# Hymba decoder step: compression weights in 2 KB runs with strided page transposes, input tiles behind earlier page units

## The chip, the core and the metric

The kernel runs on one core of one Trainium2 chip. Its engines are TensorE (PE; its weight loads are shown as PEld), VectorE (DVE), ScalarE (ACT), GpSimd (POOL) and SyncE (SP); SP, ACT and POOL also issue transfers (DMAs). The metric is device time in microseconds of one execution; lower is better. Times are compared by the medians of several executions, and the trace is of one profiled execution.

## The reference

One decoding layer for a prompt of 512 tokens and for 8 sequences of 8 new tokens, each with 2048 cached tokens in 16 pages. The layer is an adaLN-modulated RMSNorm, one input projection, attention with three branches (compressed blocks, selected blocks, window) beside a gated short convolution, an output projection and a SwiGLU network. The part that matters here is the compression of the cached keys and values, over all pages of each sequence:

```python
def compress(rows, pe, w1, w2):
    b, t = rows.shape[:2]
    r_n = CMP_LEN // CMP_STRIDE
    n_ch = t // CMP_STRIDE
    nc = n_ch - r_n + 1
    chunks = rows[:, :n_ch * CMP_STRIDE].reshape(b, n_ch, CMP_STRIDE, N_KV_HEADS, HEAD_DIM)
    chunks = chunks.transpose(0, 1, 3, 2, 4).reshape(b, n_ch, N_KV_HEADS, CMP_STRIDE * HEAD_DIM)
    proj = jnp.einsum('bnkf,rfh->rbnkh', chunks, w1.reshape(r_n, CMP_STRIDE * HEAD_DIM, CMP_HIDDEN))
    pre = sum(proj[r][:, r:r + nc] for r in range(r_n)) + pe.reshape(-1) @ w1
    return jax.nn.silu(pre) @ w2, jnp.arange(nc) * CMP_STRIDE + CMP_LEN - 1
```

`w1` is `w_ck1` for keys and `w_cv1` for values, 2048 x 64 each; `pe` is `pe_cmp`, 32 x 64; `CMP_LEN` is 32 and `CMP_STRIDE` 16 tokens.

## The kernel before

The kernel is written by hand for all five engines: each engine has one list of instructions that it runs in order, and the lists meet through semaphores. There is no planner at run time; the order in the text is the order on each engine.

**Page units.** The cached rows come in 16 units (`caches`, u = 0 to 15): for each of 8 sequences the keys (even u) and the values (odd u), 1 MB each. GpSimd fetches a unit with four indirect DMAs (L891) into one of four slots of `cring`, a part of `arena`. Before the first DMA of unit i (i at least 4) it waits until `turned` has reached i - 3, that is, until the transposes of units 0 to i - 4 have been made. VectorE then transposes the unit in blocks of 32 x 32 (`turn_chunks`, L1605, one instruction of 2048 elements a partition) into `xcmp`, of which there are two. TensorE multiplies it with `w1v` (`compress_first`, L2513: eight products that accumulate), ScalarE copies one half of the result (`second_chunks`, L1058), VectorE adds the other half (`both_chunks`, L1611), ScalarE applies SiLU (`hidden`, L1066), TensorE makes the second product (`compress_second`, L2521) and VectorE evicts it (`cmp_evac`, through L1528).

**The page loop.** For u = 0 to 15 VectorE transposes unit u + 1, evicts the second product of unit u - 2 and makes the addition for unit u. The transpose of unit u + 2 waits for TensorE's first product of unit u. Between these stand other steps: at u = 0 the evictions of the small transposed rows and of the position sums `pebt`; at u = 7 and 8 the normalisation of the input tiles; at u = 8 to 10 evictions of the transposed tiles; at u = 12 the addition of the adaLN bias (L1563); at u = 13 the modulation (L1552 to L1585, right before the addition for unit 13); at u = 14 the low part of the projection's first weights (L535). TensorE has between the units also eight steps of the adaLN product (`ada_step`, u = 4 to 11) and transposes of the input tiles. After unit 15 the input projection begins (L2445 to L2455), for which ScalarE and VectorE split weights into high and low parts.

**The position term** `pe.reshape(-1) @ w1` is made by `position_rows` after unit 0's first product: 32 products with one column each (L2501; two instruction pairs in the trace for each), with columns 36 to 51 of `colT`. These come from `pe_cmp`, which is loaded in rows of `rowb` with gains and convolution weights and transposed with them (`turn_rows`).

**Loads at the start.** ScalarE issues the identity (L1020), then `hidden_load(0)` (`w_ck1`), the gain rows, the position rows, `hidden_load(1)` (`w_cv1`), `w2` and the convolution state; only then does it run the SiLU on the condition vectors (L1049). Each `hidden_load` is eight DMAs of 64 KB, with runs of one row of 64 values (256 bytes); the row of `w1` with which partition p goes is fixed by the 32 x 32 transposes: partition 32 i + p holds feature 32 (8 i + j) + p for each j. TensorE waits for `comp_k_loaded` before unit 0 and for `comp_w_loaded` before the position sums.

SP issues the page table and the condition vectors, then the loop of L762 to L766 quoted below: it waits for page unit 2 before the first tile of x and for unit 3 before the second. `cache(eng, i)` is a wait for the four DMAs of unit i. The first four 1 MB chunks of the adaLN weights follow (L718), and then the further chunks, each behind the step that frees its place in the ring of four.

## Time and profile before

| | us |
|---|---|
| three runs | 916.96, 919.9, 920.78 |
| median | 919.9 |
| profiled execution, first to last instruction (span) | 917.5 |
| median less span (launch and what else lies around; the profiled execution's own time is not listed apart) | 2.4 |
| TensorE busy in the span | 851.0 (93%) |
| VectorE busy in the span | 624.0 (68%) |
| page stretch: first page DMA to the projection's first product | 4.15 to 127.19 |

The page is read from the top: span, busy time of each engine, then the 40 slices of the span, of which the first five or six are the page stretch. A busy share over the whole span says little here, since the page stretch and the later products have different limits; what counts for this change is which wait ends last between 4 and 127 us. In a line of the timeline the number behind the start is how long the instruction, or the row of neighbours of one kind that is merged into one line, was busy; in brackets stands how long the engine had been idle before, and what released it. "remote" means that the profile found no releaser; "issue" that the engine waited for nothing that it shows.

### The profile page before, as it was taken

Reading aid. Unit: us, or ns where it says so; the run is one execution under the profiler, and the core shown is the slowest. Engines: PE = TensorE matmul, PEld = TensorE weight load, DVE = VectorE, ACT = ScalarE, POOL = GpSimd, SP = SyncE. Lnnn points to the kernel's source line nnn. Section 1 sums busy time; section 2 is a strip of 40 time slices with the busy share of each in tenths; the row PEclk is TensorE's granted clock in tenths of the full one; section 3 lists DMA queues with packets and bytes.
Section 4 is the critical chain, followed back from the end, with each engine's and each line's share of the span. In section 5 each row is a group of like instructions: output and inputs, shape, how many; then the busy total and the mean of one; then the engine's idle time right before and its main releaser. Section 6 shows DMA issues by size and latency. Waiting matters only on the chain.

```text
span 917.5 us, 17109 instructions
## 1 busy us (share of the span) xinstructions
PE 851.0 (93%) x6685; PEld 725.8 (79%) x6685; DVE 624.0 (68%) x1220; ACT 374.3 (41%) x754; POOL 307.3 (33%) x303
## 2 busy tenths in 40 slices
PE   3499999999997789999999998999999999999998
PEld 2366778899994456776777798999999999888886
DVE  2146686388948674668485899988888888434444
ACT  1033262132135434866833664444444446323221
POOL 6456500000003311634400328766677773000000
PEclk9699999999998887999999999999999999999999
DMA  7988922237187987393102554333333324422201
GB/s 207 323 293 320 321 79 75 92 111 262 45 299 259 351 337 275 87 303 108 36 0 92 152 139 123 92 94 92 92 94 93 93 92 165 145 92 93 74 1 52
DMA packets 89167, 138.88 MB, mean 151 GB/s; under 512 B 9268, under 2 KB 59988, under 8 KB 84799
## 3 DMA queue, kind: packets, MB, share of 16 engines
q1 hardware_dynamic: 74866, 96.26, 32.6%
q0 software_dynamic: 9376, 40.31, 12.7%
q10 hardware_dynamic: 4844, 1.21, 0.6%
q8 instruction: 54, 0.88, 0.4%
q14 instruction: 27, 0.21, 0.1%
HBM read 130.58 MB, written 11.31 MB: 155 GB/s over the span
## 4 chain that ended last, share of the span: by engine, by line
PE 74%; DVE 10%; issue 8%; ACT 4%; POOL 2%; another core or an unknown queue 1%; DVEq 0%; POOLq 0%; ACTq 0%
PE bank L2445 17%; PE bank L2447 17%; PE bank L2446 16%; PE bank L2513 4%; PE bank L2439 4%; PE bank L2801 2%; PE bank L2474 2%; PE bank L2714 2%; PE bank L2933 2%; PE bank L2454 2%; PE bank L2455 2%; PE bank L2965 2%; PE bank L2771 1%; DVE ring_lo L535 1%
## 5 line engine op out<-in xcount | busy, mean ns | idle before, releaser
L2445 PE MATMUL bank<-s,ring_hi 128*128 128x288 f32 x620 | 184.1, 297 | 4.5 <-DVE ring_lo L535 4.5
L2446 PE MATMUL bank<-s,ring_lo 128*128 128x288 f32 x620 | 182.9, 295 | 0.0
L2447 PE MATMUL bank<-s,ring_hi 128*128 128x288 f32 x620 | 182.3, 294 | 0.0
L2445 PEld LDWEIGHTS bank<-s,ring_hi 128*128 128x128 f32 x620 | 116.2, 187 | 5.4 <-DVE ring_lo L535 5.3
L2447 PEld LDWEIGHTS bank<-s,ring_hi 128*128 128x128 f32 x620 | 116.8, 188 | 0.0
L2446 PEld LDWEIGHTS bank<-s,ring_lo 128*128 128x128 f32 x620 | 116.4, 188 | 0.0
L535 DVE TENSOR_TENSOR ring_lo<-mem,ring_hi 128x512 fp32r<-128x512 f32 x84 | 106.6, 1304 | 2.1 <-POOL mem L987 1.8
L535 DVE TENSOR_TENSOR dn_w<-wring,dn_w 128x2048 fp32r<-128x2048 f32 (+1 forms) x11 | 23.1, 2097 | 65.8 <-ACT dn_w L532 65.8
L2445 PE MATMUL bank<-dn_w,dn_hi 128*128 128x512 f32 x160 | 62.2, 389 | 0.0
L2446 PE MATMUL bank<-dn_w,dn_lo 128*128 128x512 f32 x160 | 62.2, 389 | 0.0
L2447 PE MATMUL bank<-dn_w,dn_hi 128*128 128x512 f32 x160 | 62.2, 389 | 0.0
L900 POOL DMA_INDIRECT arena<-in_cache_k_slc,idx x8 | 7.9, 991 | 162.0 <-PE bank L2447 152.0
L2445 PE MATMUL bank<-hhi,ws 128*128 128x288 f32 x192 | 56.8, 296 | 0.0
L2447 PE MATMUL bank<-h1hi,ws 128*128 128x288 f32 x192 | 56.6, 295 | 0.0
L2446 PE MATMUL bank<-h1hi,ws 128*128 128x288 f32 x192 | 56.5, 294 | 0.0
L532 ACT CAST dn_w<-wring 128x2048 fp32r<-128x2048 f32 (+1 forms) x11 | 19.3, 1757 | 83.0 <-PE bank L2447 83.0
L535 DVE TENSOR_TENSOR ring_lo<-wring,ring_hi 128x512 fp32r<-128x512 f32 x71 | 52.6, 746 | 0.5 <-ACT ring_hi L532 0.5
L532 ACT CAST ring_hi<-mem 128x512 fp32r<-128x512 f32 x84 | 50.0, 616 | 6.9 <-POOL mem L979 2.3
L979 POOL TENSOR_TENSOR mem<-wring 128x512 f32<-128x512 f32 x20 | 27.1, 1357 | 53.8 <-PE bank L2447 30.1
L532 ACT CAST ws<-wring 128x1024 fp32r<-128x1024 f32 (+2 forms) x18 | 21.8, 1247 | 48.4 <-PE bank L2455 27.2
L891 POOL DMA_INDIRECT arena<-in_cache_k_cmp,idq x32 | 30.6, 955 | 28.0 <-DVE uvT L1605 15.1
L532 ACT CAST ring_hi<-wring 128x512 fp32r<-128x512 f32 x71 | 39.8, 616 | 0.0
(448 smaller groups left out, 2127.4 us busy)
## 6 DMA issues: line engine op xcount, KB each, us to landing
wring<-in_w_gu SPq DMA_DIRECT2D x44, 512.0 KB
wring<-in_w_ada SPq DMA_DIRECT2D x16, 1024.0 KB
wring<-in_w_in SPq DMA_DIRECT2D x10, 1024.0 KB
wring<-in_w_down SPq DMA_DIRECT2D x10, 1024.0 KB
wring<-in_w_ada SPq DMA_DIRECT2D x16, 512.0 KB
proj<-in_x_prompt SPq DMA_DIRECT2D x4, 512.0 KB
mem<-in_state_k_win POOLq DMA_DIRECT2D x8, 256.0 KB
mem<-in_state_v_win POOLq DMA_DIRECT2D x8, 256.0 KB
```

The source lines that it names most:

```text
L532: return copy(dst, src)
L535: return eng.tensor_tensor(dst, src, hi.bitcast(F32), ALU.subtract)
L891: pool.indirect_dma_start(cring[:, slot_of(i), 512 * n:512 * n + 512], None, a[name].rearrange("l n (c i s) k d -> (l n c i) (s k d)", i=4 ...
L979: ins = pool.tensor_tensor(dst, block_of(f, 0), block_of(f, 1), ALU.subtract)
L2439: return pe.transpose(dst, src, ident[0:P, 0:P])
L2445: pe.matmul(dst, sh, ml, start=first and k == 0, stop=False)
L2446: pe.matmul(dst, sl, mh, start=False, stop=False)
L2447: ins = pe.matmul(dst, sh, mh, start=False, stop=last and k == len(pairs) - 1)
L2454: pe.matmul(dst, s, ml, start=first and k == 0, stop=False)
L2455: ins = pe.matmul(dst, s, mh, start=False, stop=last and k == len(pairs) - 1)
L2474: ins = pe.matmul(ps(key)[32 * j:32 * j + 32, :], cT[:, 32 * kk:32 * kk + 32], w[:, j, :], start=kk == 0, stop=kk == 7)
L2513: ins = pe.matmul(dst, w1v[:, u % 2, j].rearrange("p r h -> p (r h)"), x[:, j // 2, j % 2], start=j == 0, stop=j == 7)
```

## The change

1. `hidden_load(x)` becomes one DMA of 512 KB into a new place `w1_rows` (a part of `late`), with runs of 512 values (2 KB): partition p now gets the eight consecutive rows 8 p to 8 p + 7 of each half r. A new step `hidden_place(x)` on ScalarE waits for it and copies it into `w1v` in the order that TensorE reads. Both copies stand behind the SiLU on the condition vectors.
2. For this order of the features a page's values have to be transposed with a stride: element j of each run of 8 goes to product j. `turn_chunks` makes eight instructions of 256 elements a page (two for a prompt page of 512), each of which reads every eighth word. `compress_first` reads the new layout, in runs of 32 as before.
3. The position columns are loaded straight into `colT` with one DMA; `rowb` and its transpose have 36 rows instead of 52. TensorE waits for `pe_loaded` and for both copies instead of for the sixteen DMAs.
4. SP waits for page unit 0 before the first tile of x and for unit 1 before the second.

```diff
             for t in range(5):
                 if t < 2:
 
-                    cache(sp, 2 + t)
+                    cache(sp, t)
                 sp.dma_start(xs[0:TM[t], t, :], tok_rows("x_prompt", "x_sample", t)).then_inc(x_loaded[t], 16)
...
             def hidden_load(x):
 
-                w = ("w_ck1", "w_cv1")[x]
-                for r in range(2):
-                    rows = a[w][0, 1024 * r:1024 * r + 1024, :].rearrange("(i j p) h -> i p j h", i=4, j=8)
-                    for i in range(4):
-                        act.dma_start(w1v[32 * i:32 * i + 32, x, :, r, :], rows[i]).then_inc((comp_k_loaded, comp_w_loaded)[x], 16)
+                act.dma_start(w1_rows[:, x], a[("w_ck1", "w_cv1")[x]][0].rearrange("(r p j) h -> p r (j h)", r=2, j=8)
+                              ).then_inc(hidden_loaded[x], 16)
+
+            def hidden_place(x):
+
+                act.wait_ge(hidden_loaded[x], 16)
+                act.copy(w1v[:, x].rearrange("p j r h -> p r j h"), w1_rows[:, x].rearrange("p r (j h) -> p r j h", j=8)
+                         ).then_inc(hidden_placed, 1)
...
-            for r in range(2):
-                act.dma_start(rowb[36 + 8 * r:44 + 8 * r, :].rearrange("j (i p) -> j i p", i=4),
-                              bass.AP(a["pe_cmp"].tensor, 1024 * r, [[32, 8], [256, 4], [1, 32]])).then_inc(gains_loaded, 16)
+            act.dma_start(colT[:, 36:52].rearrange("p (r j) -> p r j", r=2),
+                          bass.AP(a["pe_cmp"].tensor, 0, [[8, 128], [1024, 2], [1, 8]])).then_inc(pe_loaded, 16)
...
             act.activation(scrow, crow, ACT.Silu).then_inc(scrow_ready, 1)
+            hidden_place(0)
+            hidden_place(1)
             act.wait_ge(cleared, 1)
...
-                dve.transpose(xcmp[u % 2 + (0 if u < 16 else 2)], rows).then_inc(turned, 1)
+                dst = xcmp[u % 2 + (0 if u < 16 else 2)]
+                for n in range(CR if u < 16 else 1):
+                    for k in range(2):
+                        c = slice(512 * n + 256 * k, 512 * n + 256 * k + 256)
+                        ins = dve.transpose(dst[:, c], rows[:, 512 * n:512 * n + 512].rearrange("p (s k d j) -> p k j s d", s=4, k=2, d=8)[:, k])
+                ins.then_inc(turned, 1)
...
             def position_rows():
 
-                pe.wait_ge(comp_w_loaded, 160)
+                pe.wait_ge(pe_loaded, 16)
+                pe.wait_ge(comp_w_loaded, 32)
+                pe.wait_ge(hidden_placed, 2)
...
-                x = xcmp[u % 2 + (0 if u < 16 else 2)].rearrange("p (n s k e r) -> p s e k n r", s=4, k=2, e=2, r=32)
+                x = xcmp[u % 2 + (0 if u < 16 else 2)].rearrange("p (n k j r) -> p j k n r", k=2, j=8, r=32)
                 dst = ps(key)[:, 0:2 * n].rearrange("p (k n r) -> p k n r", k=2, r=32)
                 for j in range(8):
-                    ins = pe.matmul(dst, w1v[:, u % 2, j].rearrange("p r h -> p (r h)"), x[:, j // 2, j % 2], start=j == 0, stop=j == 7)
+                    ins = pe.matmul(dst, w1v[:, u % 2, j].rearrange("p r h -> p (r h)"), x[:, j], start=j == 0, stop=j == 7)
...
                 if u == 0:
                     turn_rows()
-                    pe.wait_ge(comp_k_loaded, 128)
+                    pe.wait_ge(hidden_placed, 1)
                 compress_first(u)
```

## Rows read from the trace of the kernel before

**Rows 1.** Page head and list of queues: packets, MB, share of 16 engines.

```profile
span 917.5 us, 17109 instructions
...
q10 hardware_dynamic: 4844, 1.21, 0.6%
```

**Rows 2.** Timeline, units 12 to 15: start, us, engine, line, op, [idle before <-releaser].

```profile
106.74 2.30 DVE L1605 STREAM_TRANSPOSE uvT<-arena 128x2048 f32<-128x2048 f32 x1
109.19 3.69 PE L2513 MATMUL bank<-uvT,mem 128*128 128x256 f32 x16 [0.44 <-DVE uvT L1605]
109.47 2.28 DVE L1605 STREAM_TRANSPOSE mem<-arena 128x2048 f32<-128x2048 f32 x1
113.72 2.30 DVE L1605 STREAM_TRANSPOSE uvT<-arena 128x2048 f32<-128x2048 f32 x1
120.21 0.41 DVE L1611 TENSOR_TENSOR arena<-arena,bank 64x254 f32<-64x254 f32 x1
120.54 2.30 DVE L1605 STREAM_TRANSPOSE mem<-arena 128x2048 f32<-128x2048 f32 x1
127.19 0.50 PE L2445 MATMUL bank<-ws,h1hi 128*128 128x512 f32 x1
```

**Rows 3.** Timeline of the first 42 us: transposes, position sums, unit 0's copy.

```profile
13.22 2.31 DVE L1605 STREAM_TRANSPOSE uvT<-arena 128x2048 f32<-128x2048 f32 x1 [9.30 <-DMA arena<-in_cache_k_cmp,idq]
15.02 1.05 ACT L1049 ACTIVATE hbuf<-hbuf 9x1024 f32<-9x1024 f32 x1
18.50 2.31 DVE L1605 STREAM_TRANSPOSE mem<-arena 128x2048 f32<-128x2048 f32 x1 [2.97 <-DMA arena<-in_cache_v_cmp,idq]
22.48 0.80 PE L2501 MATMUL bank<-colT,mem 128*64 128x1 f32 x21
38.40 0.37 ACT L1058 COPY arena<-bank 64x254 f32<-64x254 f32 x1 [22.33 <-remote]
41.02 2.30 DVE L1605 STREAM_TRANSPOSE uvT<-arena 128x2048 f32<-128x2048 f32 x1
```

**Rows 4.** Timeline: GpSimd's restarts after pauses, and ScalarE's two later long waits.

```profile
43.58 0.95 POOL L891 DMA_INDIRECT arena<-in_cache_k_cmp,idq  x1 [9.43 <-DVE uvT L1605]
66.42 0.37 ACT L1058 COPY arena<-bank 64x254 f32<-64x254 f32 x1 [9.48 <-remote]
69.80 0.95 POOL L891 DMA_INDIRECT arena<-in_cache_k_cmp,idq  x1 [5.69 <-DVE uvT L1605]
88.95 1.39 POOL L891 DMA_INDIRECT arena<-in_cache_v_cmp,idq  x1 [4.31 <-DVE mem L1605]
104.86 0.37 ACT L1058 COPY arena<-bank 64x254 f32<-64x254 f32 x1 [5.16 <-remote]
```

**Rows 5.** Groups by form on VectorE: shapes xcount | busy us, mean ns | idle.

```profile
L1605 DVE STREAM_TRANSPOSE uvT<-arena 128x2048 f32<-128x2048 f32 x8 | 18.4, 2298 | 9.3 <-DMA arena<-in_cache_k_cmp,idq 9.3
L1605 DVE STREAM_TRANSPOSE uvT<-wring 128x512 f32<-128x512 f32 x2 | 1.4, 712 | 0.1
L1796 DVE TENSOR_REDUCE uvT<-uvT 127x32 f32<-127x128 f32 x4 | 1.5, 373 | 1.5 <-ACT uvT L1178 1.5
L1693 DVE TENSOR_REDUCE hss<-mem 64x2 f32<-64x128 f32 x2 | 0.6, 278 | 0.1
L1528 DVE COPY mem<-bank 127x128 f32<-127x128 f32 x16 | 4.0, 252 | 0.0
L1563 DVE TENSOR_TENSOR arows<-bank,arows 128x512 f32<-128x512 f32 x3 | 2.0, 670 | 0.0
```

**Rows 6.** Timeline: DMA issues of ScalarE's first weight, and of SP's input tiles.

```profile
1.17 4.13 ACTq L1028 DMA_DIRECT2D mem<-in_w_ck  x8
21.79 8.27 SPq L766 DMA_DIRECT2D proj<-in_x_prompt  x4
```

**Rows 7.** Stretches: busy us of PE, PEld, DVE, ACT, POOL; clock; DMA share; GB/s.

```profile
10.00:15.00 5.00, 0.00 (x0) 0.00 (x0) 1.78 (x1) 1.28 (x1) 3.78 (x5) 1.00 1.07 240
45.00:50.00 5.00, 5.00 (x25) 4.00 (x23) 2.81 (x3) 1.92 (x4) 3.29 (x4) 1.00 1.02 418
```

More of the change, by code:

```diff
@@ L326, in decoder_kernel @@
         w1v = att[:, 0:2048].rearrange("p (x j r h) -> p x j r h", x=2, j=8, r=2)
+        w1_rows = late[:, 0:2048].rearrange("p (x r n) -> p x r n", x=2, r=2)
         kT = [z.rearrange("p (s k e n) -> p k e s n", s=16, k=2, e=2) for z in (att[:, 0:2048], hbuf[:, 0:2048])]
@@ L342, in decoder_kernel @@
         spare = 5 * TEND
-        rowb = proj[0:52, spare:spare + 128]
+        rowb = proj[0:36, spare:spare + 128]
         winb = mem[:, 4 * TOK:4 * TOK + 2048]
@@ L1623, in _ @@
                          ps(("cT",))[:, 0:72].rearrange("p (k r) -> p k r", r=9))
-                    evac(("rows",), colT[:, :], ps(("rows",))[:, 0:52])
+                    evac(("rows",), colT[:, 0:36], ps(("rows",))[:, 0:36])
                     for x in range(2):
@@ L2486, in turn_rows @@
                 fills(ins, ("cT",))
-                pe.wait_ge(gains_loaded, 112)
+                pe.wait_ge(gains_loaded, 80)
                 want_free(pe, ("rows",))
-                fills(turn(ps(("rows",))[:, 0:52], rowb[:, :]), ("rows",))
+                fills(turn(ps(("rows",))[:, 0:36], rowb[:, :]), ("rows",))
             def position_rows():
-                pe.wait_ge(comp_w_loaded, 160)
+                pe.wait_ge(pe_loaded, 16)
+                pe.wait_ge(comp_w_loaded, 32)
+                pe.wait_ge(hidden_placed, 2)
                 want_emptied(pe, ("cT",))
```

5 lines of the change are left out of this document (3 added, 2 removed).

## The prediction

> **What bounds the kernel now.** I read three views in this order. First the page's head and queue list, for the span and for what the weight loads cost the DMA engines [rows 1]: the execution spans 917.5 us, 2.4 below the median of the three runs (919.9), so the sum below is made on the span and 2.4 is added at the end. Second the timeline of the stretch before the input projection. All edits lie in it, and from the projection's first product at 127.19 on [rows 2] TensorE runs a fixed program, so a later start moves the end by as much. What releases that start is a chain through VectorE: the page transposes of units 12 to 15 (T12 to T15 below) start at 106.74, 109.47, 113.72 and 120.54, and T15 is followed by the last compression and then the projection [rows 2]. Third the timeline of the start and of GpSimd's waits, since it is not VectorE's work that made T12 as late as 106.74. TensorE begins the position sums at 22.48, yet ScalarE gets the result of page unit 0 only at 38.40, after 22.33 us of waiting whose releaser the profile cannot name, and VectorE starts T2 at 41.02 [rows 3]. GpSimd runs out of free ring slots meanwhile and takes up unit 6 at 43.58; the same picture returns at 66.42 and 104.86, with GpSimd pauses before 69.80 and 88.95 [rows 4]. I call these the stalls. Each ends about when GpSimd has paused. I do not know their mechanism, and the rivals turn on it.
>
> **The transposes.** One instruction of 2048 elements a page becomes eight of 256, which read every eighth word. Price by rows [rows 5]: 2048 elements take 2298 ns and 512 take 712, so 1.033 ns an element and 183 ns fixed; neighbours overlap by 0.08 (an addition of 0.41 is followed after 0.33 [rows 2]). Were the stride free, a page would cost 8 x (183 + 264) - 7 x 80 = 3.02 us. No transpose in this trace reads with a stride. The nearest row is the reduction at L1796, which reads 128 elements with just this stride of eight words: 373 ns, where a dense reduction of 128 takes 278. That is 0.74 ns more an element, and the page costs 8 x (183 + 264 + 190) - 560 = 4.54 us. If the whole 373 ns grow with the elements (2.91 each), it is 5.97. I take 4.54, by the nearest row: 2.24 more a page, 36 us more over 16 pages, all on VectorE. Below zero is excluded: eight instructions move the same elements.
>
> The Trainium skill (Vector Engine (DVE) Microarchitecture Reference, section 5.2, measured stream behaviour) says that a port streams at full rate only in runs of two or more adjacent 4-byte words; it gives about 1.7 ns a column for far hops on each element and 2.5 for small steps. The row gives 1.78 in all, so it agrees with the first figure; by the second a page would cost about 6 us, an estimate, which is the rival "dear stride". The rule speaks against this change.
>
> **Where the added time falls.** In the middle of the stretch it has cover. VectorE's own cycle becomes 4.54 + 0.42 = 4.96 us a page (the transpose, an eviction of 0.25 and an addition of 0.41, less three overlaps). Ten pages lie between T2 and T12; without the two stalls of 9.48 and 5.16 they take now (106.74 - 41.02 - 14.64) / 10 = 5.11 each [rows 3, 4], and GpSimd needs (88.95 - 4.31 - 69.80) / 3 = 4.95 a unit. So VectorE becomes as slow as the others, not slower. What has no cover: GpSimd's unit 6 is released by T2, which ends 2.24 later. The next two restarts (69.80, 88.95) hang on T6 and T9 in the same way, so if the stalls return in full the lag grows to 6.7; if they go, up to 14.6 come back. I take 2.2 at T12 and nothing for the others.
>
> The tail has no cover either [rows 2, 5]. Counted from T12's present start: T13 ends at 106.74 + 4.46 + 4.54 = 115.74. An eviction (0.25), the bias addition (0.67) and the addition of the halves (0.41) follow, about 1.2 with overlaps, and T14 starts at 116.9; now it starts at 113.72, behind TensorE's unit 12 (109.19 + 3.69), which would end at 115.1 and no longer decides. From T14's end to the addition at 120.21 it takes 4.19 now (modulation), and that stays: 116.9 + 4.54 + 4.19 + 0.33 = 125.96 for T15, which ends at 130.5 instead of 122.84. **Tail: 7.7 us.** The two prompt pages read 512 elements: two instructions cost 2 x 637 - 80 = 1.19 against 0.71, 1.0 for both, among TensorE products; 0 to 1.0, I take 0.5.
>
> **The weight loads.** Sixteen ScalarE issues of 0.52 us (eight in 4.13 [rows 6]) and two of the position rows become three, so ScalarE's SiLU moves up by some 7 us from 15.02 [rows 3]. ScalarE's queue takes 0.6% of 16 engines over the span, 5.5 us of the DMA engines in all, for 1.21 MB [rows 1]; in the stretch from 10 to 15 they are full at 240 GB/s, where from 45 to 50 they move 418 [rows 7]. So the long runs can give at most about 3 us of DMA time (1.21 MB at 418 GB/s is 2.9 us) to the first pages: T0 starts at 13.22, T1 at 18.50, both on landings [rows 3]. It is worth nothing at T2, since the stall to 38.40 lies between. New on ScalarE are two waits for the landed weights and two copies of 1024 elements a partition, each like the SiLU row's 1.05. They stand before the wait that opens the page loop; behind them are queued only unit 0's copy (38.40), and SiLU has already run. TensorE's first compression waits for the first copy, but T0 now ends at 17.8, later than both. The position sums need T1's followers: 18.50 + 4.54 + 0.3 = 23.3 against 22.48. That is 0.8 us, hidden if the stall stays, lost if it goes. The position columns landed directly and the two shorter operations on them cost nothing while they land before 23.
>
> **The input tiles.** SP's first x load waits for unit 0 (about 13.2) and the second for unit 1 (18.5), instead of units 2 and 3; they issue from 21.79 now [rows 6]. Behind them on SP stand the other x loads and four weight chunks of 1 MB, which all move up by about 6 us. Nobody waits for these (ScalarE's first square on x comes after 41). They compete earlier with units 2 to 5, whose transposes wait for the stall anyway. Cost and gain zero; if the stall goes, a page delayed by 0.5 MB at 418 GB/s costs 1.3.
>
> **Sum:** 2.2 + 7.7 + 0.5 = 10.4 us; 917.5 + 10.4 = 927.9, and with the 2.4 around it **930**. Its own range runs from 922 (part of the later stalls gone) to 937 (lag 6.7 and one more).
>
> **Rivals.**
> Stall gone: the first stall is caused by the load of short packets or by where the x loads fall, and the change removes it. Then the position sums (21 of 64 pairs took 0.80 [rows 3], so all 2.4) end at 25.7, T2 starts at 26.4 instead of 41.02, 14.6 earlier; with the tail's 7.7 and 0.5 that is -6.4, or **914**, and down to 905 when the later stalls shrink too. It decides as soon as more than 10.4 us of the 14.6 come back. For it: the DMA engines are full at a low rate in just that stretch [rows 7]. Against it: the stalls at 66.42 and 104.86 come long after the short packets are gone, and GpSimd's run of 24 issues to 34.15 (43.58 less its wait of 9.43) is as long as before.
> Stride free: the transpose's read does not pay for hops. A page costs 3.02, 0.72 more: 0.7 at T2, and in the tail 0.7 + 0.7 + 0.8 = 2.2, so about +3: **923**. For it: L1796 is another kind of instruction.
> Dear stride: 5.97 a page. 3.7 at T2, the tail by the same steps 13.4, prompt pages 1, and VectorE's cycle of 6.4 is slower than the 5.11 of the stretch, by 12.8 over ten pages that the stalls absorb or not: +18 to +31, **938 to 951**. For it: the skill's second figure.
> That the loads of weights and tiles do not move up at all would change nothing in the sum, since neither is waited for.
>
> **How the numbers follow.** About 0.5% (4.6 us) is what a measurement here can tell from no change. Forecast 0.48 (of it 0.04 inside 0.5%), stall gone 0.26 (a little of it below 906), stride free 0.15, dear stride 0.11. Faster 0.26, same 0.19, slower 0.55. The range leaves out the dear stride beyond 941 and the lowest part of "stall gone": 906 to 941; the likeliest case alone has 922 to 937.
>
> **What would show it.** Right: eight transposes a page of about 0.64 us each, T15 ending 23 to 25 us after T12's start (16.1 now), ScalarE's copy of unit 0 still near 38. Stall gone: that copy near 23 and GpSimd without its 9.43 pause. Stride free: transposes of 0.45. Wrong altogether if the projection's start and the end move by different amounts, or if TensorE waits for the hidden weights.

## The result: slower by 0.44%, less than half of what was forecast

Over 20 executions each the kernel before has a median of 921.65 us and the kernel after 924.58; the ratio is 1.0044, with a 95% interval of 1.0026 to 1.0063, so about 4 us more (the two medians lie 2.9 apart, the means 3.9). The forecast was 10.4 more. The direction and the range held, the size did not. By the forecast's own bound of 0.5% this is "no change", for which it gave 0.19.

| | before | after |
|---|---|---|
| median, us | 921.65 | 924.58 |
| lowest and highest | 916.05, 924.58 | 920.1, 931.22 |
| span of the profiled execution | 917.5 | 923.7 |
| T12 starts | 106.74 | 101.04 |
| T15 ends | 122.84 | 124.18 |
| projection's first product | 127.19 | 129.94 |
| from there to the end | 790.3 | 793.8 |

The groups of VectorE after the change, by form (instructions, busy us, mean ns), answer to [rows 5]:

```profile
L1615 DVE STREAM_TRANSPOSE mem<-arena 128x256 f32<-128x256 f32 x64 | 34.5, 607 | 2.0 <-DMA arena<-in_cache_v_cmp,idq 2.0
L1615 DVE STREAM_TRANSPOSE uvT<-arena 128x256 f32<-128x256 f32 x64 | 34.5, 607 | 7.7 <-DMA arena<-in_cache_k_cmp,idq 7.7
L1615 DVE STREAM_TRANSPOSE uvT<-wring 128x256 f32<-128x256 f32 x4 | 2.4, 650 | 0.1
```

One strided transpose takes 607 ns, and eight in a row 4.25 to 4.39 us: the 4.54 of the sum, nearly. The four of the prompt pages (last line) take 2.4 us where two took 1.4, the upper end of the sum's 0 to 1.0; what they add to the whole time was not told apart. The timeline of the last pages (from T11 on) answers to [rows 2]:

```profile
95.95 4.36 DVE L1615 STREAM_TRANSPOSE mem<-arena 128x256 f32<-128x256 f32 x8
98.81 0.37 ACT L1064 COPY arena<-bank 64x254 f32<-64x254 f32 x1 [3.08 <-issue]
101.04 4.34 DVE L1615 STREAM_TRANSPOSE uvT<-arena 128x256 f32<-128x256 f32 x8
105.78 4.30 DVE L1615 STREAM_TRANSPOSE mem<-arena 128x256 f32<-128x256 f32 x8
111.08 4.32 DVE L1615 STREAM_TRANSPOSE uvT<-arena 128x256 f32<-128x256 f32 x8
119.93 4.25 DVE L1615 STREAM_TRANSPOSE mem<-arena 128x256 f32<-128x256 f32 x8
124.33 5.10 PE L2526 MATMUL bank<-mem 128*128 128x256 f32 x16 [3.01 <-DVE mem L1615]
129.94 0.50 PE L2456 MATMUL bank<-ws,h1hi 128*128 128x512 f32 x1
```

From T12's start to T15's end it is 23.1 us (16.1 before): the tail costs 7.0. But T12 starts 5.7 earlier than before, where the sum had it 2.2 later: from T11 to T12 it takes 5.1 us, and before the change 9.2 (T11 at 97.58). And unit 15's products take 5.10 us, behind 3.01 us in which TensorE had nothing to do, where 16 of them took 3.69 in [rows 2]. The start of the stretch answers to [rows 3] and [rows 4]:

```profile
8.91 1.98 ACT L1032 COPY mem<-arena 128x1024 f32<-128x1024 f32 x2
11.64 4.25 DVE L1615 STREAM_TRANSPOSE uvT<-arena 128x256 f32<-128x256 f32 x8 [7.72 <-DMA arena<-in_cache_k_cmp,idq]
17.91 4.29 DVE L1615 STREAM_TRANSPOSE mem<-arena 128x256 f32<-128x256 f32 x8 [2.02 <-DMA arena<-in_cache_v_cmp,idq]
22.57 1.06 PE L2514 MATMUL bank<-colT,mem 128*64 128x1 f32 x30 [0.21 <-DVE colT L1534]
25.43 0.16 PE L2514 MATMUL bank<-colT,mem 128*64 128x1 f32 x1 [1.79 <-issue]
26.90 0.37 ACT L1064 COPY arena<-bank 64x254 f32<-64x254 f32 x1 [16.02 <-issue]
38.03 1.66 PE L2514 MATMUL bank<-colT,mem 128*64 128x1 f32 x27 [1.24 <-issue]
40.25 4.29 DVE L1615 STREAM_TRANSPOSE uvT<-arena 128x256 f32<-128x256 f32 x8
44.81 0.94 POOL L893 DMA_INDIRECT arena<-in_cache_k_cmp,idq  x1 [10.64 <-DVE uvT L1615]
...
63.59 0.37 ACT L1064 COPY arena<-bank 64x254 f32<-64x254 f32 x1 [5.54 <-issue]
68.93 0.95 POOL L893 DMA_INDIRECT arena<-in_cache_k_cmp,idq  x1 [2.66 <-DVE uvT L1615]
75.62 0.95 POOL L893 DMA_INDIRECT arena<-in_cache_v_cmp,idq  x1 [1.98 <-DVE mem L1615]
87.06 0.37 ACT L1064 COPY arena<-bank 64x254 f32<-64x254 f32 x1 [4.40 <-remote]
94.64 0.95 POOL L893 DMA_INDIRECT arena<-in_cache_k_cmp,idq  x1 [2.17 <-DVE uvT L1615]
```

The loads do what they should: both weights lie in place at 10.9, T0 starts 1.6 earlier. T2 doesn't notice. Thirty of the 64 instruction pairs of the position sums run at once, then TensorE gets single steps, with 1.1 to 2.6 us of idle time between, until at 38.03 the last 27 follow in 1.66 us. T2 starts at 40.25 (41.02 before). The later waits of ScalarE are shorter than before: 5.54 us for the 9.48 at 66 [rows 4], 4.40 for one of 8.05 at 85, 3.08 for the 5.16 at 105 [rows 4]. GpSimd's pauses behind 50 are shorter too, up to 2.66.

### The profile page after: what moved, and what is told of

Read it like the earlier page. It is cut to its first block, busy times and chain, and to the rows that moved or that the text cites. A ratio compares the mean times of both kernels' runs of the same rounds, so it can differ in the third digit from the quotient of the medians.

```text
span 923.7 us, 17211 instructions
## 1 busy us (share of the span) xinstructions
PE 856.7 (93%) x6685; PEld 733.8 (79%) x6685; DVE 645.6 (70%) x1334; ACT 376.2 (41%) x756; POOL 322.4 (35%) x303
## 4 chain that ended last, share of the span: by engine, by line
PE 75%; DVE 14%; issue 7%; ACT 2%; POOL 1%; another core or an unknown queue 0%; DMA 0%; DVEq 0%; ACTq 0%; POOLq 0%
PE bank L2456 18%; PE bank L2458 17%; PE bank L2457 17%; PE bank L2450 4%; DVE mem L1615 3%; PE bank L2814 2%; DVE uvT L1615 2%; PE bank L2727 2%; PE bank L2946 2%; PE bank L2465 2%; PE bank L2466 2%; PE bank L2784 2%; PE bank L2526 2%; PE bank L2978 2%; PE bank L2485 1%
## 5 line engine op out<-in xcount | busy, mean ns | idle before, releaser
L537 DVE TENSOR_TENSOR ring_lo<-mem,ring_hi 128x512 fp32r<-128x512 f32 x84 | 91.4, 1107 | 23.4 <-POOL mem L989 23.1
L537 DVE TENSOR_TENSOR dn_w<-wring,dn_w 128x2048 fp32r<-128x2048 f32 (+1 forms) x11 | 23.1, 2097 | 65.8 <-ACT dn_w L534 65.8
L537 DVE TENSOR_TENSOR ring_lo<-wring,ring_hi 128x512 fp32r<-128x512 f32 x71 | 60.0, 850 | 0.5 <-ACT ring_hi L534 0.5
L981 POOL TENSOR_TENSOR mem<-wring 128x512 f32<-128x512 f32 x20 | 31.5, 1577 | 43.7 <-DVE s L537 23.7
L2526 PE MATMUL bank<-uvT,mem 128*128 128x256 f32 (+1 forms) x160 | 36.1, 382 | 6.2 <-DVE uvT L1615 5.7
```

Of the source, the lines that this page charges most:

```text
L537: return eng.tensor_tensor(dst, src, hi.bitcast(F32), ALU.subtract)
L981: ins = pool.tensor_tensor(dst, block_of(f, 0), block_of(f, 1), ALU.subtract)
L2526: ins = pe.matmul(dst, w1v[:, u % 2, j].rearrange("p r h -> p (r h)"), x[:, j], start=j == 0, stop=j == 7)
```

## The experiments

All kernels in one table, from one profiled execution each; the ratio to the kernel before is from all executions. "Rest" is the span from the projection's first product to the end.

| kernel | ratio, 95% interval | T2 | T12 | projection | span | rest |
|---|---|---|---|---|---|---|
| before | 1 | 41.02 | 106.74 | 127.19 | 917.5 | 790.3 |
| after | 1.0044, 1.0026 to 1.0063 | 40.25 | 101.04 | 129.94 | 923.7 | 793.8 |
| x_order_alone | 0.9983, 0.9962 to 1.0004 | 40.62 | 104.56 | 126.90 | 919.1 | 792.2 |
| without_x_order | 1.008, 1.0051 to 1.011 | 40.64 | 104.66 | 133.68 | 931.0 | 797.3 |
| strided_alone | 1.0089, 1.0058 to 1.0119 | 40.91 | 106.96 | 137.38 | 930.4 | 793.0 |
| one_transpose | 0.9975, 0.9952 to 0.9998 | 40.54 | 105.15 | 125.60 | 914.8 | 789.2 |
| two_dense | 1.0014, 0.9981 to 1.0047 | 40.60 | 110.20 | 134.14 | 925.6 | 791.5 |
| eight_dense | 1.0075, 1.005 to 1.01 | 39.88 | 110.55 | 132.25 | 922.1 | 789.9 |
| two_strided | 1.0051, 1.0023 to 1.0078 | 40.25 | 103.40 | 131.75 | 920.5 | 788.8 |
| busy_before_u15 | 1.0061, 1.003 to 1.0092 | 40.48 | 106.67 | 135.12 | 925.1 | 790.0 |
| sums_first | 1.0071, 1.0044 to 1.0099 | 45.58 | 107.40 | 137.24 | 926.3 | 789.1 |
| slots3 | 0.9948, 0.9926 to 0.9969 | 35.13 | 99.55 | 119.99 | 911.7 | 791.7 |
| slots2 | 0.9964, 0.994 to 0.9988 | 29.48 | 98.28 | 123.54 | 914.9 | 791.4 |
| slots3_alone | 0.9968, 0.9939 to 0.9996 | 35.41 | 100.06 | 127.17 | 915.6 | 788.4 |
| slots3_after | 1.0025, 0.9997 to 1.0052 | 35.26 | 102.55 | 133.51 | 921.8 | 788.3 |
| half_pages | one execution | 41.15 | 110.44 | 134.06 | 928.9 | 794.8 |
| one_issue | 1.0054, 1.0034 to 1.0073 | 52.17 | 108.10 | 131.60 | 923.5 | 791.9 |
| one_issue_after | 0.9817, 0.9778 to 0.9857 | 25.45 | 81.77 | 111.79 | 904.0 | 792.2 |
| one_issue_dense | 0.9813, 0.9771 to 0.9855 | 23.27 | 82.71 | 106.21 | 899.9 | 793.7 |

Two readings of the table hold throughout. The rest is 788 to 797 whatever the page stretch does, with no trend against the projection's start, which runs from 106 to 137: a later start moves the end, with a scatter of some 9 us that lies behind it. And one profile of a kernel says little: busy_before_u15 and after differ only behind unit 14, yet T12 is at 106.67 in the one and at 101.04 in the other (T5 at 56.34 and 56.40, T6 at 69.43 and 64.40), and the rest is 790.0 in the one and 793.8 in the other. So of the 6.2 us between the two profiled spans of before and after, the 3.5 behind the projection's start are not shown to come from the change.

### The parts of the change

x_order_alone is the kernel before with one line changed:

```diff
-                    cache(sp, 2 + t)
+                    cache(sp, t)
```

> The kernel before with the fourth part of the change alone: the input tiles begin behind page units 0 and 1. The trace after the change has T12 at 101.04 instead of 106.74, although every page costs 2.1 us more on VectorE. Theory X: the input tiles and the first four weight chunks, issued some 10 us earlier, no longer fall on the later pages, and that is what took the stalls before 66 and 105 down. Then this kernel has the 5.7 us and no dearer transposes: T12 at 95 to 101, the projection's first product at 115 to 121, and a ratio of 0.987 to 0.994 to the kernel before. Theory P: it is VectorE's slower pace itself that spreads the pages. Then the stalls stay and the ratio is 0.998 to 1.002. Theory L (the longer runs of the compression weights): also 0.998 to 1.002.

Measured: 0.9983, an interval that includes no change; T12 at 104.56, 2.2 earlier, of which 0.3 is left at the projection. Theory X falls: T12 is not at 95 to 101, nor the ratio at 0.994 or less.

without_x_order is the kernel after with this line put back.

> The kernel after the change with the fourth part undone: the input tiles begin behind page units 2 and 3 again. Theory X: the later stalls return, T12 comes at 106 to 109 and the ratio to the kernel before is 1.008 to 1.012 (my forecast of 10.4 us). Theories P and L: T12 stays near 101 and the ratio stays at 1.003 to 1.006.

Measured: 1.008, as theory X had it, but T12 at 104.66. Against the whole change (1.0044) the earlier input tiles are worth 3.3 us (0.0036 of 921; 0.1 to 6.5 with both intervals), alone 1.6 (nothing to 3.5).

strided_alone puts only the eight strided transposes into the kernel before:

```diff
-                dve.transpose(xcmp[u % 2 + (0 if u < 16 else 2)], rows).then_inc(turned, 1)
+                dst = xcmp[u % 2 + (0 if u < 16 else 2)]
+                for n in range(CR if u < 16 else 1):
+                    for k in range(2):
+                        c = slice(512 * n + 256 * k, 512 * n + 256 * k + 256)
+                        ins = dve.transpose(dst[:, c], rows[:, 512 * n:512 * n + 512].rearrange("p (s k d j) -> p k j s d", s=4, k=2, d=8)[:, k])
+                ins.then_inc(turned, 1)
```

> The kernel before with the strided transposes alone: eight instructions of 256 elements a page, two for a prompt page, each reading every eighth word. Weights, position columns and input tiles are loaded as before, so the products meet the wrong features and everything computed from the compressed keys and values differs. By my forecast's sum the long weight runs and the input tiles are worth nothing, so this kernel alone should cost the whole 10.4 us: ratio 1.009 to 1.013. If the runs of 2 KB give something at the start, it is slower than the change without the input tiles (1.008): 1.010 or more. If the slower VectorE spaces the pages and so shortens the later stalls by itself, T12 to the projection is some 7 us longer than before but T12 itself comes 1 to 6 us earlier: 1.003 to 1.008.

Measured: 1.0089, or 8.2 us, with an interval of 5.3 to 11.0: it holds the 10.4 that the whole change was forecast to cost. Against it the whole change gives some 4 back (0.8 to 7.4).

one_transpose is the kernel after with the opposite edit:

```diff
-                for n in range(CR if u < 16 else 1):
-                    for k in range(2):
-                        ...
+                ins = dve.transpose(dst, rows)
```

> The kernel after the change, but each page transposed again by one instruction of 2048 elements without a stride (256 for a prompt page is 512 again); its products therefore meet the wrong features, and everything computed from the compressed keys and values differs. This is parts 1, 3 and 4 of the change without the dearer transposes. The last four pages should take 16 us again instead of 23.1. Theories X and L: T12 at 95 to 101 or earlier and the projection at 115 to 122, a ratio of 0.987 to 0.995. Theory P: with the fast transposes the stalls are back, the projection at 126 to 128, and the ratio 0.998 to 1.001.

Measured: 0.9975, so weights, position columns and input tiles together are worth 2.3 us (0.2 to 4.4). The forecast had zero. T12 is at 105.15, not before 101, so what came earlier in the profile of after (101.04) isn't due to these loads alone. Against this kernel the strided transposes cost 6.4 us (1.0044 less 0.9975; 3.6 to 9.1).

### How many instructions, and which reads

```diff
 eight_dense
-                for n in range(CR if u < 16 else 1):
-                    ...
+                for n in range(2 * CR if u < 16 else 2):
+                    ins = dve.transpose(dst[:, 256 * n:256 * n + 256], rows[:, 256 * n:256 * n + 256])
 two_strided
-                ...
+                for k in range(2):
+                    c = rows.shape[1] // 2
+                    ins = dve.transpose(dst[:, c * k:c * k + c], rows.rearrange("p (s k d j) -> p k j s d", k=2, d=8, j=8)[:, k])
...
-                x = xcmp[u % 2 + (0 if u < 16 else 2)].rearrange("p (n k j r) -> p j k n r", k=2, j=8, r=32)
+                x = xcmp[u % 2 + (0 if u < 16 else 2)].rearrange("p (k j n r) -> p j k n r", k=2, j=8, r=32)
 two_dense
-                ...
+                c = rows.shape[1] // 2
+                for k in range(2):
+                    ins = dve.transpose(dst[:, c * k:c * k + c], rows[:, c * k:c * k + c])
```

> The kernel after the change, but the eight transposes of a page each read 256 neighbouring words (two for a prompt page); the features are mixed up, so what is computed from the compressed keys and values differs. This tells the stride from the count of instructions. By my sum eight dense ones cost 3.02 us a page (2.30 for the single one, 4.3 measured with the stride): T12 to T15's end 17 to 19 us, and the projection's first product between the 125.6 of the single transpose and the 129.94 of the change, near 127. Ratio 0.997 to 1.002. If instead the count of instructions is what costs (a page near 4.3 us), the ratio is 1.003 to 1.006.

> The kernel after the change with two strided transposes of 1024 elements a page instead of eight of 256 (the four quarters of a page can be walked as one dimension when the result is laid out by product instead of by quarter; the products read the new order, and the result is the reference's). It asks whether the count of instructions on VectorE is what costs, since eight dense ones took only 2.71 us a page (0.41 more than one) and yet cost 0.0100 of the time. From the rows so far, 607 ns strided and 401 dense for 256, a page should take 2 x 137 + 2048 x 1.84 = 4.04 us (4.3 with eight). Theory N (the count costs, by instructions that come late to the engines while GpSimd issues): most of the gap between one and eight transposes goes, ratio 0.997 to 1.001. Theory S (the strided read costs its own time, as in my sum): only 0.3 us a page less, about 1 us in the tail, ratio 1.002 to 1.005.

> The kernel after the change with two dense transposes of 1024 elements a page. Eight dense ones (2.71 us a page) cost 9 us against one (2.30), more than their own time of 0.41 a page allows in a tail of four pages. If that is the count of instructions, two cost next to nothing: ratio 0.996 to 0.999. If already 0.1 us a page and one more instruction bring the later stalls into another rhythm, the ratio is 1.001 or more, and the kernels' differences of a few us say little on the transposes' own price.

In two_dense, as in eight_dense, the products meet the wrong features; so they do in one_issue_dense below.

The groups by form of VectorE, first eight_dense:

```profile
L1613 DVE STREAM_TRANSPOSE uvT<-arena 128x256 f32<-128x256 f32 x64 | 21.7, 401 | 8.1 <-DMA arena<-in_cache_k_cmp,idq 7.9
```

then two_strided:

```profile
L1614 DVE STREAM_TRANSPOSE mem<-arena 128x1024 f32<-128x1024 f32 x16 | 31.5, 2004 | 2.7 <-DMA arena<-in_cache_v_cmp,idq 2.7
```

and two_dense:

```profile
L1614 DVE STREAM_TRANSPOSE uvT<-arena 128x1024 f32<-128x1024 f32 x16 | 18.9, 1214 | 7.9 <-DMA arena<-in_cache_k_cmp,idq 7.8
```

These settle the price: strided (2004 - 607) / 768 = 1.82 ns an element, dense (1214 - 401) / 768 = 1.06, fixed 141 and 130 ns. The stride costs 0.76 ns an element (0.74 in the sum, from the reduction in [rows 5]). The rivals "dear stride" (2.91 ns, 5.97 us a page) and "stride free" (3.02 us a page) are refuted. The Trainium skill (Vector Engine (DVE) Microarchitecture Reference, section 5.2, measured stream behaviour) gives about 1.7 ns a column where one stream hops far on each element, and 2.5 where both sources or the result go in steps of 24 words; the 1.82 measured here, for a read alone in steps of 8 words, is about 0.1 above the first.

They don't settle the time. A page costs 2.30, 2.35, 2.71, 3.93 and 4.3 us with one dense, two dense, eight dense, two strided and eight strided transposes; the ratios are 0.9975, 1.0014, 1.0075, 1.0051, 1.0044. Both theory N and the plain price fall: eight dense transposes are not cheaper than strided ones. In their profile T12 is at 110.55, 5.4 later than with one. Something else moves T12, by 9.5 us from the earliest profile to the latest.

### What ends the first stall

sums_first moves the position sums ahead of unit 0 and takes their two waits for evictions away:

```diff
+                    position_rows()
                 compress_first(u)
-                if u == 0:
-                    position_rows()
```

> The kernel after the change with the 32 position sums moved ahead of unit 0's first product (the position columns land directly now, so they need no transposed row any more); TensorE is idle there from about 13 to 16 us. Theory F: in the stretch from 23 to 38 us TensorE gets one instruction every 0.7 us whatever it does, so what counts is how many instructions stand there; 64 pairs less let T2 start at 24 to 28 instead of 40.25, and GpSimd goes on without its pause before 44.81. Then T12 is 5 to 15 us earlier and the ratio to the kernel before is 0.987 to 0.999. Rival: the starved stretch only moves to the next instructions (unit 1's products and ScalarE's), T2 starts at 36 to 41 as now, and the ratio stays at 1.003 to 1.006.

Both expectations fell. TensorE's timeline in sums_first:

```profile
11.07 2.37 PE L2512 MATMUL bank<-colT,mem 128*64 128x1 f32 x41 [0.71 <-issue]
...
38.10 0.59 PE L2512 MATMUL bank<-colT,mem 128*64 128x1 f32 x7 [1.24 <-issue]
38.63 6.05 PE L2524 MATMUL bank<-uvT,mem 128*128 128x256 f32 x16
```

The single steps now begin ten microseconds earlier, at 13.4 after 41 pairs, and still end at 38.1. Unit 0's products stand behind them, and T2 comes at 45.58. So the stretch doesn't begin at a fixed time, but it ends at one: 37.8 to 38.4 in every kernel with four slots and four transfers a unit.

slots3 and slots2 hold GpSimd to three and two units ahead (with the input tiles behind units 0 and 1); slots3_alone leaves the input tiles as before, and slots3_after has the limit in the kernel after:

```diff
-                if i >= CR:
-                    pool.wait_ge(turned, i - CR + 1)
+                if i >= 3:
+                    pool.wait_ge(turned, i - 3 + 1)
```

> The kernel before with the input tiles begun behind units 0 and 1, and with GpSimd held to three page units ahead instead of four (unit i waits until unit i - 3 is transposed, from i = 3 on). It asks what ends the starved stretch that ends at 38.0 to 38.3 in every kernel so far. Theory G: TensorE, ScalarE and VectorE get few instructions while GpSimd issues page transfers, and the stretch ends some 4 us after GpSimd stops. With three slots GpSimd stops at 29.2 instead of 34.15, so the position sums end and T2 starts about 5 us earlier (35 to 36 instead of 40.6), and the ratio is 0.990 to 0.998. Theory D (the transfers of input tiles and the first weight chunks fill the DMA engines until then): the stretch still ends at 36 to 38, and with one slot less the kernel is no faster: 0.998 to 1.006.

> The same with two page units ahead. Theory G: GpSimd issues units 0 and 1 until 14.2, unit 2 behind T0 (15.5) and unit 3 behind T1 (22), and then stops at about 27 until T2: the position sums start at 22.5 and suffer only until 27 to 31, T2 starts at 28 to 32. Later GpSimd never runs ahead, so the waits of 5 to 9 us before 67 and 84 shrink as well, but each unit now starts only behind a transpose: 5 us of issue, about 2 of landing and 2.3 of transpose over two units, at most 5 us a unit, as now. Ratio 0.985 to 1.000. Theory D: T2 at 36 or later, and the later units slower: 1.005 to 1.03.

The timeline of slots3:

```profile
32.29 2.20 PE L2501 MATMUL bank<-colT,mem 128*64 128x1 f32 x38 [1.23 <-issue]
35.13 2.30 DVE L1605 STREAM_TRANSPOSE uvT<-arena 128x2048 f32<-128x2048 f32 x1
37.70 0.94 POOL L891 DMA_INDIRECT arena<-in_cache_v_cmp,idq  x1 [8.60 <-DVE uvT L1605]
```

and of slots2:

```profile
28.50 0.16 PE L2501 MATMUL bank<-colT,mem 128*64 128x1 f32 x1 [1.14 <-issue]
32.05 0.95 POOL L891 DMA_INDIRECT arena<-in_cache_k_cmp,idq  x1 [4.78 <-DVE uvT L1605]
```

GpSimd stops at 37.70 - 8.60 = 29.1 and at 27.3 instead of 34.15, and the sums come free at 32.3 and 28.5 instead of 38.3. In slots2 50 of the 64 pairs run at once from 22.68, while GpSimd issues, and the broken steps begin only behind them. Theory G holds, theory D falls: the end follows GpSimd's stop by 1 to 4 us. slots3 is 0.9948, some 5 us faster than the kernel before and 9 faster than the one after, with nothing left out; slots2 (0.9964) starts sooner, but waits for landings later (T3 at 37.76, T4 at 46.66).

> The kernel before with three page units ahead, input tiles behind units 2 and 3 as in the kernel before. If the limit on GpSimd alone makes the gain of 5 us, the ratio is 0.992 to 0.998 and T2 starts near 35. If the earlier input tiles are half of it, the ratio is 0.996 to 1.001.

Measured 0.9968, T2 at 35.41: the limit alone makes 2.9 of the 4.8 us, and with intervals as wide as these the two kernels are not told apart. Both expectations hold this ratio; T2 is as the first had it.

> The kernel after the change with GpSimd held to three page units ahead. It asks what the change costs where the stalls are shorter. The first starved stretch should end near 32.4 (38.03 with four slots), T2 start at 34 to 35. If the dearer transposes cost what the last four pages show (7 us) and little is given back elsewhere, it is 6 to 10 us slower than the kernel before with the input tiles moved and three slots (0.9948): ratio 1.000 to 1.006. If the slower VectorE gives back by itself what the shorter queue of pages gives, the two gains don't add: 1.003 to 1.006, as without the limit.

Measured 1.0025, T2 at 35.26: against slots3 (0.9948) the transposes and weight loads of the change cost 7.1 us (3.9 to 10.3), as the first expectation had it.

half_pages and one_issue tell bytes from issues (half_pages transposes the loaded half twice, by two instructions of 1024 elements a page):

```diff
 half_pages
-  cring[:, slot_of(i), 512 * n:512 * n + 512], None, a[name].rearrange("l n (c i s) k d -> (l n c i) (s k d)", i=4, s=4)
+  cring[:, slot_of(i), 512 * n:512 * n + 256], None, a[name].rearrange("l n (c i s) k d -> (l n c i) (s k d)", i=8, s=2)
...
 one_issue
-  ...
+  cring[:, slot_of(i), :], None, a[name].rearrange("l n (c s) k d -> (l n c) (s k d)", s=16), ... idx[:, b:b + 1]
```

> The kernel before with every page transfer cut to half its bytes (128 rows of 1 KB instead of 2 KB, as many transfers and issues as before; the rows are others, and each half is transposed twice by two instructions of 1024 elements a page, so that what is computed from the compressed keys and values differs). It asks what starves TensorE while GpSimd issues. If it is GpSimd's issuing itself, or the count of packets, the position sums still end at 37 to 39 and ScalarE's next steps with them, and the pauses stay as long. If it is the bytes of the pages that fill the DMA engines (1.02 of their share from 30 to 40 in the kernel after), half the bytes end the stretch at 24 to 31.

The timeline of half_pages shows the stretch unmoved:

```profile
38.43 2.09 PE L2508 MATMUL bank<-colT,mem 128*64 128x1 f32 x36 [1.26 <-issue]
43.78 0.95 POOL L891 DMA_INDIRECT arena<-in_cache_k_cmp,idq  x1 [9.68 <-DVE uvT L1608]
```

With half the bytes the DMA engines are not full until 30, and TensorE has single steps all the same (columns as in [rows 7]):

```profile
25.00:30.00 5.00, 0.42 (x2) 0.54 (x3) 0.00 (x0) 0.00 (x0) 3.78 (x5) 0.53 0.66 231
```

> The kernel before with one page transfer a unit instead of four: GpSimd issues one indirect transfer of 128 rows of 8 KB, the same 1 MB (the rows land on other partitions, so what is computed from the compressed keys and values differs). The counterpart of the half pages, which had all the issues and half the bytes and left the starved stretch as it was, to 38.43. Theory G: it is GpSimd's issuing (or the count of its packets). Then the first four units are issued by about 10, GpSimd stops there, the position sums run through without single steps, T2 starts at 24 to 28 instead of 41.02, the later waits of 5 to 9 us are gone, and units come every 4.5 us: projection at 90 to 110, ratio 0.965 to 0.985. Theory B (the bytes in flight, or the units taken together): the stretch to 38 stays, T2 at 36 to 41, ratio 0.99 to 1.01.

one_issue has no single steps (64 of 64 pairs in a row), and of ScalarE's later waits over 3 us each has a named releaser. Its sums run when GpSimd is not issuing (nothing between 17.8 and 54.7). But its start is bad for another reason, as its timeline shows:

```profile
7.85 18.31 ACTq L1028 DMA_DIRECT2D mem<-in_w_cv  x8
47.85 3.58 PE L2501 MATMUL bank<-colT,mem 128*64 128x1 f32 x64 [3.14 <-DMA proj<-in_w_cv]
```

With the pages coming faster, ScalarE needs 18.31 us for the eight issues of the second weight in its short runs, and SiLU, the first products and the sums wait for that. This is what the change repairs, so the last pair has the change and one transfer a unit, strided and with one dense transpose.

> The kernel after the change with one page transfer a unit (as one_issue; the rows land on other partitions, so what is computed from the compressed keys and values differs). In one_issue the later stalls were gone (T2 to T15 took 72.8 us, 79.5 in the kernel before, every wait on named work), but the start was worse: ScalarE needed 18.31 us to issue the second compression weight, eight transfers of short runs, behind full DMA engines, and T2 came at 52.17. If that is what the long runs of the change are for, the start is repaired here: position sums at 20 to 24, T2 at 24 to 28, then 13 pages at 5.0 to 6.0 us: projection at 100 to 113, ratio 0.968 to 0.985. If the weights are not what delays T2, it stays at 40 to 52 and the ratio at 0.995 to 1.010.

The timeline of one_issue_after:

```profile
4.34 0.49 ACTq L1026 DMA_DIRECT2D arena<-in_w_cv  x1
22.68 2.03 PE L2514 MATMUL bank<-colT,mem 128*64 128x1 f32 x64
25.45 4.29 DVE L1615 STREAM_TRANSPOSE uvT<-arena 128x256 f32<-128x256 f32 x8
```

and the stretch in which its sums run, with the DMA engines full and GpSimd at one issue:

```profile
20.00:25.00 5.00, 5.00 (x76) 4.25 (x75) 1.27 (x6) 0.37 (x1) 0.94 (x1) 1.00 1.01 421
```

So full DMA engines alone do not make the single steps. All as the first case had it: the issue takes 0.49, the 64 pairs run in 2.03, T2 starts at 25.45, and the ratio is 0.9817 where one_issue had 1.0054. Under this condition weights, position columns and input tiles bring 0.0237, or 22 us, in spite of the dearer transposes. In the kernel before, the same eight issues take 3.84 us (from 8.01) and T2 stands behind the stall; there the loads are worth the 2 to 4 us above.

> The same with one dense transpose of 2048 a page: the price of the strided transposes where GpSimd starves nobody. By my sum's steps: 7 us in the last four pages, and between T2 and T12 whatever VectorE's cycle of 4.7 us exceeds TensorE's and GpSimd's. So it should be 7 to 15 us faster than one_issue_after. If the price is hidden there too (TensorE the bound, 4.2 us a page and the adaLN steps), 0 to 4 us.

Measured 0.9813, 2 us less than its strided partner (903.66 and 905.73, four executions each, so not told apart). In the profiles the projection starts 5.6 earlier and the span is 4.1 shorter: 6.5 less from T12 to the projection, 0.9 lost before it, where the dense kernel waits for an adaLN weight chunk (3.22 us at 42). Less than the 7 to 15 expected; the 0 to 4 of the second case hold it.

### Unit 15's products

```diff
+                if u == 15:
+                    for j in range(6):
+                        pe.matmul(ps(key)..., w1v[:, 0, j]..., spare_x[:, j], start=True, stop=True)
                 pe.wait_ge(turned, u + 1)
```

> The kernel after the change with six more of unit 15's products (twelve instructions of TensorE, about 2.8 us, on the other buffer, overwritten afterwards) in the 3.01 us in which TensorE waits for the last transpose. It asks whether that idle time is what slows unit 15's own products from 3.7 to 5.10 us at a granted clock of 0.78 to 0.88. If so, they take 3.7 to 3.9 here, the granted clock from 120 to 130 is 1.00, and the projection starts 5.7 us minus 1.3, some 4.4 to 4.6 us, after T15's end less 0.1 (5.76 in the kernel after). If not, 5.1 remains. The time is 1.3 us shorter in the first case, which three rounds will hardly show: ratio 1.001 to 1.006 either way.

The stretches of the kernel after (busy us of PE, PEld, DVE, ACT, POOL; granted clock; DMA share; GB/s):

```profile
120.00:125.00 5.00, 1.39 (x7) 1.13 (x7) 5.00 (x11) 2.02 (x4) 0.00 (x0) 0.88 0.00 0
125.00:130.00 5.00, 5.00 (x21) 3.95 (x19) 3.87 (x7) 2.98 (x5) 0.00 (x0) 0.78 0.40 115
```

The timeline of busy_before_u15:

```profile
127.86 2.86 PE L2525 MATMUL bank<-uvT,mem 128*128 128x256 f32 x12
130.88 3.72 PE L2531 MATMUL bank<-mem 128*128 128x256 f32 x16 [0.17 <-DVE mem L1615]
```

and two of its stretches:

```profile
125.00:130.00 5.00, 4.39 (x22) 3.57 (x21) 5.00 (x11) 2.02 (x4) 0.00 (x0) 1.00 0.00 0
130.00:135.00 5.00, 4.83 (x24) 3.71 (x22) 4.93 (x9) 1.40 (x3) 0.00 (x0) 1.00 0.13 19
```

With TensorE kept at work the granted clock stays at 1.00 (the level of 2.4 GHz), the products take 3.72 instead of 5.10, and the projection starts 4.29 us after T15's end instead of 5.76. So behind the idle 3.01 us the products take 1.4 more, at a clock that is at the level of 1.2 GHz for part of the stretch (0.88 and 0.78 in the mean). The whole kernel shows nothing of it (1.0061 against 1.0044, with overlapping intervals).

## Why the prediction was right in sign and wrong in size

**What bounds the kernel** was right. The end follows the start of the projection in all 19 kernels, within the scatter of the rest, and the stalls, not VectorE's work, make T12 late. The sign that the prediction set against itself, that the projection's start and the end move by different amounts, did come in the profiled pair (2.8 and 6.2); the scatter of the rest is enough for it.

**The price of a page** was right: 4.3 against 4.54, with 0.76 ns for the stride against 0.74 and a fixed part of 0.14 against 0.18.

**The tail** was nearly right: 7.0 to T15's end against 7.7, plus 1.4 for unit 15's products that were not in the sum. In the five kernels with strided transposes and four slots (sums_first, with its other order, left out; after, without_x_order, strided_alone, two_strided, busy_before_u15) T12 to projection takes 28.3 to 30.4, in their five dense counterparts (before, x_order_alone, one_transpose, two_dense, eight_dense) 20.5 to 23.9; the means differ by 7.3.

**The failed step** is the term at T12, "I take 2.2 at T12 and nothing for the others": it let every stall return as it was, only later. T12 is not later with the dearer transposes. Its mean is 104.5 in the five strided kernels (101.0 to 107.0) and 107.4 in the five dense ones (104.6 to 110.6). The ranges overlap, since the earlier stalls vary from profile to profile; but the last stall, between T11 and T12, tells the two kinds apart. In the kernel before GpSimd passes to unit 14 almost without a pause:

```profile
94.85 0.95 POOL L891 DMA_INDIRECT arena<-in_cache_k_cmp,idq  x1 [0.68 <-issue]
97.58 2.30 DVE L1605 STREAM_TRANSPOSE mem<-arena 128x2048 f32<-128x2048 f32 x1
```

ScalarE then waits 5.16 us (at 104.86 in [rows 4]), and T12 comes 9.2 us after T11. In the kernel after GpSimd has to wait 2.17 us there for the longer transpose T10 (the line at 94.64 above), ScalarE's wait is 3.08 us, what it also is in one_issue, whose later pages have no stalls, and T12 comes 5.1 after T11. So it is in the others:

| | T11 to T12, us | GpSimd's pause before unit 14, us |
|---|---|---|
| after, without_x_order, strided_alone, two_strided, busy_before_u15 | 5.1, 5.1, 5.1, 4.7, 5.5 | 2.2, 2.2, 2.1, 1.8, 2.1 |
| before, one_transpose, two_dense, eight_dense | 9.2, 9.2, 10.6, 10.6 | 0.7 or less |
| x_order_alone | 6.1 | 4.5 |

In the other nine kernels it is the same: where GpSimd pauses for 1.8 us or more between 5 us before T11 and T12, it takes 5.0 to 5.8 from T11 to T12, and in slots3, the one without such a pause, 10.5. So the dearer transposes pay for a part of themselves: they make GpSimd wait, and this stall does not come. Up to T11 the strided kernels are 1.1 later in the mean, and from T11 to T12 they win 4.0, which makes the 2.9; 7.3 - 2.9 gives 4.4 at the projection, and by their medians the five strided kernels are 5.1 slower than the five dense ones. The prediction named this end (up to 14.6 back when the stalls shrink) and gave it no place in the likeliest case. What is read from the traces here is which pause goes with which stall; no run changes this one pause alone.

**"Worth nothing"** for weight loads and input tiles is a second term that failed, by medians no smaller: together 2.3 us (0.2 to 4.4) with one transpose, and some 4 as the difference between strided_alone and after. Pairs of kernels that differ by the transposes give 6.4 us (one_transpose to after) and 8.2 (before to strided_alone), where the sum had 10.4: so by medians the transposes were taken 2 to 4 us too dear and the loads 2 to 4 us too low. T2 gained only 0.8, as foreseen, and for the reason foreseen: the first stall lies between. What was not known is that the same loads are worth 22 us once GpSimd issues one transfer a unit.

**The rivals.** "Stall gone" did not happen: GpSimd's pause is 10.64 (9.43 in [rows 4]). Its sign in the profile was ill chosen: ScalarE's copy of unit 0 did move, to 26.90, and in one_transpose to 20.02, while the sums stayed where they were; the position sums and T2 are the sign. That the short packets or the place of the input tiles cause the stall is refuted by one_transpose and x_order_alone, where the sums still come free at 38.4 and 38.0. "Stride free" and "dear stride" are refuted by the durations, and that the measured time comes out near the 923 of the former is a coincidence.

**Still open:** by what way GpSimd's issuing keeps instructions from TensorE and ScalarE (one_issue has fewer issues, and also fewer, longer packets, and its sums fall where GpSimd is not issuing; up to 41 us GpSimd's queue has 1856 packets in the kernel before, 864 in one_issue and 1151 in half_pages, which keeps the single steps, so the packets are the less likely cause), why the single steps begin only after some 50 pairs and more, and why eight dense transposes, 0.4 us a page dearer than one, brought T12 5 us later.

## What to carry to other kernels

When several engines idle together with no named releaser and GpSimd is issuing indirect transfers without a pause, first ask how many issues stand in a row: a shorter queue of units (three slots for four) took 5 us off here. One larger transfer a unit took off 17 (0.9817) together with the loads of the change and nothing without them (1.0054), in kernels whose page rows land on other partitions and give other results; a version with the right results was not tried. A gain at a stage that ends in such a stall may not be seen until the stall is gone, and a loss beside one can be partly paid by it; a sum that keeps the stalls fixed can be wrong in both directions. And when T12 moves by 5 us between two profiles of the same work, judge a part of the change by the median of many executions and read the profile for durations.

## What the runs showed of the hardware

While GpSimd issued page transfers four units ahead, TensorE ran 51 to 62 instruction pairs from the program's begin and then started single ones, mostly at multiples of about 0.70 us (1.24 us idle and 0.16 of work make 1.40, 1.94 and 0.16 make 2.10; two steps in the kernel before do not fit, 3.60 and 2.35). With two units ahead it ran 80 pairs first. This ended 1 to 4 us after GpSimd's stop. Half the bytes with as many issues changed nothing (38.43); a quarter of the issues, with the same bytes and about half the packets, removed it (64 pairs in 2.03 us, with the DMA engines full at 421 GB/s). In one_issue, whose pages filled the DMA engines (share 0.97 to 1.05 from 10 to 30), eight issues of 64 KB in runs of 256 bytes held ScalarE for 18.31 us, where eight such issues take 4.13 at the start [rows 6] and one issue of 512 KB in runs of 2 KB takes 0.49. A transpose of 32 x 32 blocks took 1.06 ns an element for adjacent words and 1.82 for every eighth word, with 130 to 141 ns fixed.
